# Gate products in three bf16 passes and weight rings of four tiles in a two-layer encoder with expert retrieval

## What is computed

```python
h = rmsnorm(x, norm_ffn[l]) * (1.0 + sc2) + sh2        # h: 256 x 1024
q = (h @ w_q).reshape(t, 8, 2, 128)                    # 8 heads, 2 sides
sc = einsum('thpd,hpnd->thpn', q, sub_keys)            # 128 keys a side
v1, i1 = top_k(sc[:, :, 0], 16); v2, i2 = top_k(sc[:, :, 1], 16)
cand = v1[..., :, None] + v2[..., None, :]             # 16 x 16 a head
top_v, top_pos = top_k(cand, 16)                       # expert = i1 * 128 + i2
gates = softmax(top_v)
a = gelu(einsum('tkd,td->tk', u_tab[eidx], x)) * gates
out = einsum('tk,tkd->td', a, v_tab[eidx])             # 16384 experts in u, v
x = x + g2 * out
```

## Time and profile before

| | us |
|---|---|
| median of 3 runs | 2061.69 |
| lowest and highest | 2059.86, 2061.74 |
| the profiled execution | 2065.37 |
| its span, first to last instruction | 2063.4 |
| mean granted TensorE clock | 0.987 of full speed |

### The profile page before, as it was taken

One profiled execution on the slowest core, in us unless ns is written; L12 is line 12 of the kernel. 1 busy time (PEld: TensorE's weight loads), 2 busy tenths in 40 slices (PEclk: granted clock), 3 DMA queues, 4 the chain that ended last, 5 costly groups with the idle time before them and its releaser, 6 DMA issues.

```text
span 2063.4 us, 43464 instructions
## 1 busy us (share of the span) xinstructions
PE 2018.4 (98%) x12678; PEld 1805.7 (88%) x12678; DVE 1487.8 (72%) x3743; ACT 1054.8 (51%) x2059; POOL 27.7 (1%) x56
## 2 busy tenths in 40 slices
PE   7989999999999999999999999999999999999997
PEld 6748899999999877777779689999999998888886
DVE  5662778877777688888875348786777767777776
ACT  2032245755555555555544424566555555555554
POOL 0000000000000000000000000000000000000000
PEclk9999999999999999999989999999999999999998
DMA  9861288865655899999820333777565577777774
GB/s 377 343 236 46 87 279 288 251 189 177 175 171 175 277 325 327 322 328 323 279 102 31 154 117 121 229 219 212 172 176 175 171 207 245 242 240 241 241 242 150
DMA packets 170904, 446.79 MB, mean 217 GB/s; under 512 B 19024, under 2 KB 85840, under 8 KB 166880
## 3 DMA queue, kind: packets, MB, share of 16 engines
q1 hardware_dynamic: 163472, 392.65, 59.6%
q0 software_dynamic: 7376, 53.45, 6.6%
HBM read 409.32 MB, written 36.70 MB: 216 GB/s over the span
## 4 chain that ended last, share of the span: by engine, by line
PE 94%; ACT 2%; DVE 2%; DMA 1%; issue 1%; DVEq 0%; ACTq 0%; SPq 0%
PE bank L492 93%; ACT big L931 1%; DMA big<-in_w_mod 1%; PE bank L631 1%; DVE raw L1097 0%; DVE big L1192 0%; PE bank L811 0%; DMA cst<-in_consts 0%; DVE big L1114 0%; DVE wmod_ring L1114 0%; DVE x_lo L1106 0%; DVE big L1527 0%; ACT L991 0%; ACT big L949 0%; ACT raw L878 0%
## 5 line engine op out<-in xcount | busy, mean ns | idle before, releaser
L1356 DVE TENSOR_TENSOR lo<-raw,hi 128x512 fp32r<-128x512 f32 x1024 | 702.5, 690 | 346.4 <-ACT hi L985 342.1
L985 ACT ACTIVATE hi<-raw 128x512 fp32r<-128x512 f32 x1024 | 642.8, 630 | 444.1 <-PE bank L492 430.2
L492 PE MATMUL bank<-x_hi,hi 128*128 128x256 f32 x2152 | 622.2, 289 | 3.9 <-ACT x_hi L876 1.8
L492 PE MATMUL bank<-x_hi,lo 128*128 128x256 f32 x2152 | 610.1, 283 | 0.0
L492 PE MATMUL bank<-x_lo,hi 128*128 128x256 f32 x2152 | 606.1, 283 | 0.0
L492 PEld LDWEIGHTS bank<-x_hi,hi 128*128 128x128 f32 x2152 | 413.6, 192 | 6.8 <-issue 4.2
L492 PEld LDWEIGHTS bank<-x_hi,lo 128*128 128x128 f32 x2152 | 413.6, 192 | 0.0
L492 PEld LDWEIGHTS bank<-x_lo,hi 128*128 128x128 f32 x2152 | 411.7, 192 | 0.0
L492 PE MATMUL bank<-hi,a_hi 128*128 128x512 f32 x1024 | 401.3, 392 | 3.4 <-issue 1.7
L492 PE MATMUL bank<-hi,a_lo 128*128 128x512 f32 x1024 | 398.8, 389 | 0.0
L492 PE MATMUL bank<-lo,a_hi 128*128 128x512 f32 x1024 | 398.4, 389 | 0.0
(11 more groups left out here) (159 smaller groups left out, 1344.4 us busy)
## 6 DMA issues: line engine op xcount, KB each, us to landing
raw<-in_u SPq DMA_DIRECT2D x256, 512.0 KB, 3.9
raw<-in_v SPq DMA_DIRECT2D x256, 512.0 KB, 4.6
s_store<-work SPq DMA_DIRECT2D x256, 128.0 KB, 3.7
wmod_ring<-s_store SPq DMA_DIRECT2D x256, 128.0 KB, 3.7
wmod_ring<-in_w_mod SPq DMA_DIRECT2D x54, 512.0 KB, 5.7
big<-in_w_mod SPq DMA_DIRECT2D x40, 512.0 KB, 6.3
big<-in_w_q POOLq DMA_DIRECT2D x16, 1024.0 KB, 7.1
big<-in_w_in POOLq DMA_DIRECT2D x6, 2048.0 KB, 14.4
```

Of the source, the lines that this page charges most:

```text
L492: return nc.tensor.matmul(o, w, x, start=start, stop=stop, skip_group_check=free)
L985: f(hi[:, r % 2, c], raw[:, r, c], ACT.Copy).then_inc(s[l]["hi_done"], 1)
L1356: v.tensor_tensor(lo[:, r % 2, c], raw[:, r, c], hi[:, r % 2, c].bitcast(F32), ALU.subtract).then_inc(s[l]["lo_done"], 1)
```

## The change

1. **Gate products in bf16.** The gate of each token is written as a sum of three bf16 numbers (`gate_bf`), indices are kept in bf16 (`pick_bf`). VectorE writes the one-hot of the second index for four tokens with the token innermost (`hot_second`), the one-hot of the first in bf16 (`hot_first`), and `hot_second` times the three parts (`hot_gate`, 1536 elements). TensorE multiplies three times for each token, reading `hot_gate` with a step of four elements. `iota4` is a constant that is written once.
2. **Rings of four tiles.** `hi` and `lo` are four deep, and split and remainder work on whole tiles of 1024, three tiles ahead of TensorE's use in the ring. `advance` after each remainder has 1000 (300 with a dot product) in place of twice 500.
3. **Layer 1's projection.** The first three tiles are multiplied in plain fp32; `x_hi` and `x_lo` are made beside them, and only then the split tiles follow.
4. **Layer 0's first weights.** The first piece of w_in is halved: 1 MB after four dot products, 1 MB after 15, the next piece after 16.
5. POOL's DMA scratch is set to 2048 bytes.

```diff
-SPLITS = 2
+SPLITS = 4
+PLAIN_TILES = 3
-                    for n in range(4):
-                        last = mm(bank[b][:, n * P:(n + 1) * P], hot[b % 2][:, 0, n, :], hot[b % 2][:, 1, n, :])
+                    for n in range(4):
+                        for c in range(3):
+                            last = mm(bank[b][:, n * P:(n + 1) * P], hot_first[b % 2][:, n, :], hot_gate[b % 2][:, c, :, n], c == 0, c == 2)
...
-                        v.tensor_scalar(hot[r % 2][:, 1, n, :], iota, pick[:, 1, bass.ds(4 * g + n, 1)],
-                                              pick[:, 2, bass.ds(4 * g + n, 1)], ALU.is_equal, ALU.mult)
+                    if again:
+                        dve.wait_ge(s[l]["hot_ready"], g)
+                    v.tensor_tensor(hot_second, iota4, pick_bf[:, 1, bass.ds(4 * g, 4)].unsqueeze(1).to_broadcast([P, P, 4]), ALU.is_equal)\
+                        .then_inc(s[l]["hot_plain"], 1)
+                    v.tensor_tensor(hot_first[r % 2], iota.unsqueeze(1).to_broadcast([P, 4, P]),
+                                    pick_bf[:, 0, bass.ds(4 * g, 4)].unsqueeze(2).to_broadcast([P, 4, P]), ALU.is_equal)
+                    dve.wait_ge(s[l]["hot_plain"], g + 1)
+                    v.tensor_tensor(hot_gate[r % 2], hot_second.unsqueeze(1).to_broadcast([P, 3, P, 4]),
+                                    gate_bf[:, :, bass.ds(4 * g, 4)].unsqueeze(2).to_broadcast([P, 3, P, 4]), ALU.mult)\
+                        .then_inc(s[l]["hot_ready"], 1)
...
-                def split(n, r, h, round_, wait=True):
+                def split(n, r, round_, wait=True):
-                        act.wait_ge(s[l]["w_used"], 2 * n + h - 3)
-                    c = slice(h * HALF, (h + 1) * HALF)
-                    f(hi[:, r % 2, c], raw[:, r, c], ACT.Copy).then_inc(s[l]["hi_done"], 1)
+                        act.wait_ge(s[l]["w_used"], n - 3)
+                    f(hi[:, r], raw[:, r], ACT.Copy).then_inc(s[l]["hi_done"], 1)
...
-                    split(n + 2, nr, 0, nround)
+                    split(n + 3, (r + 3) % 4, round_ + (r + 3) // 4, wait or r > 0)
                     gelu(n, r, round_, wait)
-                    split(n + 2, nr, 1, nround)
...
                     weigh(j + 2, (r + 2) % 4, round_ + (r + 2) // 4)
-                    for half in range(2):
-                        lower(NKEY + 2 + j, (r + 2) % 4, half)
+                    if left:
+                        lower(NKEY + 3 + j, (r + 3) % 4)
                     lower_a(j + 2, r, (r + 2) % 4)
...
-                    sp.wait_ge(s[l]["lo_done"], STREAM - 6 + 2 * j)
+                    sp.wait_ge(s[l]["lo_done"], NKEY - 3 + j)
                     load_v(j, r)
                     if fetches:
                         fetch(j + 1, (r + 1) % 4, i + (1 if r == 3 else 0))
...
+                for m in range(PLAIN_TILES):
+                    weights_in(m)
+                    for k in range(KT):
+                        if m == 0:
+                            pe.wait_ge(norms["h_ready"], KT * 2 + k + 1)
+                        last = mm(bank[m][:, 0:T], w_qk(1, m, k), hT[:, k, :], k == 0, k == KT - 1)
+                    last.then_inc(s[1]["wt_used"], 1)
+                pe.wait_ge(s[1]["ph_done"], KT)
+                pe.wait_ge(s[1]["pl_done"], KT)
```

More of the change, by code:

```diff
@@ L183, in build @@
         fox_maps = wmod_ring[:].rearrange("p a n -> p (a n)")
-        hot = [x.rearrange("p (a t n) -> p a t n", a=2, n=P) for x in (wmod_ring[:, 0], wmod_ring[:, 1])]
+        hot_first = [ring[:, n * D:n * D + 256].bitcast(BF16).rearrange("p (t n) -> p t n", t=4) for n in range(2)]
+        hot_gate = [ring[:, n * D + 256:(n + 1) * D].bitcast(BF16).rearrange("p (a n t) -> p a n t", a=3, t=4) for n in range(2)]
         back = wmod_ring[:, 2].rearrange("p (r t) -> p r t", t=T)
@@ L1406, in experts @@
                         for n in range(2):
-                            for half in range(2):
-                                lower(n, n, half)
+                            lower(n, n)
                 for n in range(GROUP_AT - 2):
-                    for half in range(2):
-                        lower(n + 2, (n + 2) % 4, half)
-                        if l == 0 and half and n % MIX_STEP == 0 and n < MIX_STEP * MIXED_MODS:
-                            mixed_modulation(n // MIX_STEP)
-                        else:
-                            advance(500)
+                    lower(n + 2, (n + 2) % 4)
+                    if l == 0 and n % MIX_STEP == 0 and n < MIX_STEP * MIXED_MODS:
+                        mixed_modulation(n // MIX_STEP)
+                        advance(300)
+                    else:
+                        advance(1000)
                 for _ in left:
@@ L1432, in experts @@
                     for r in range(4):
-                        for half in range(2):
-                            lower(4 * i + r, r, half)
+                        lower(4 * i + r, r)
                 dve.wait_ge(s[l]["g_copied"], GROUPS)
@@ L1438, in experts, with down_step @@
                 for n in range(2):
-                    for half in range(2):
-                        lower(NKEY + n, n, half)
+                    lower(NKEY + n, n)
                     lower_a(n, n, n)
-                def down_step(j, r, round_, mods=None):
+                lower(NKEY + 2, 2)
+                def down_step(j, r, round_, mods=None, left=True):
                     weigh(j + 2, (r + 2) % 4, round_ + (r + 2) // 4)
-                    for half in range(2):
-                        lower(NKEY + 2 + j, (r + 2) % 4, half)
+                    if left:
+                        lower(NKEY + 3 + j, (r + 3) % 4)
                     lower_a(j + 2, r, (r + 2) % 4)
```

300 lines of the change are left out of this document (138 added, 162 removed).

## The result

| | before | after |
|---|---|---|
| median of the runs, us | 2061.72 (4 runs) | 2154.31 (4 runs) |
| lowest and highest | 2059.86, 2063.20 | 2148.68, 2158.88 |
| ratio of the medians, 95% interval | | 1.0448, 1.0422 to 1.0475 |
| span of the profiled execution | 2063.4 | 2152.5 |
| granted TensorE clock | 0.987 | 0.992 |

A forecast was written before the change was run, and what follows sets the result against it. TensorE, busy 98% of the span, was taken as the bound. Terms -16.1 - 8 - 2.6 - 2 = -28.7 us took the profiled 2065.4 to 2036.7; the median being 3.7 lower, 2033.0 us was predicted, range 2016 to 2064.

The forecast's parts named there:

- gate products: Gate steps on TensorE: 12 bf16 matmuls at 0.057 us replace 8 fp32 records, -16.1 us (ends -26 and +68).
- VectorE in the gate step: Gate step: VectorE needs 2.9 us at doubled bf16 pace, stays hidden behind TensorE's 3.63 us, costs nothing.
- ring, layer 0's down stage: Layer 0's down stage: four-deep ring bridges the dot-product gaps, -8 us (ends -11.8 and +4).
- start of layer 1: Layer 1's projection: three plain fp32 tiles let TensorE begin at once, -2.6 us (-0.9 to -4.3, depending on the clock).
- up to the first gate product: Start of layer 0: halved first w_in load leaves room for modulation weights, -2 us (ends 0 and -2.5).
- the picks' row: Profile row of 64 bf16 matmuls of 128 columns, 0.057 us each, taken as the pace of the new gate matmuls.
- Rival (c): Layer 0's down stage: late loads stall four tiles 1 us instead of 0.4, +19 us, total 2060 us; 6 in 100.
- if this stays: Layer 1's projection: if TensorE stays at 1.2 GHz in part, denser work loses 3.4 us, only 0.9 gained.
- (a): Gate step: the twelve matmuls run slower, halfway at 0.085 us, +14.3 us in all, 2076 us; 11 in 100.
- the far part of (a): Gate step: matmul spacing above about 0.077 us, which the predicted range left out.

The follow-up runs named there:

- both repairs: Changed kernel with two tokens innermost in the gate operand (4-byte step) and SyncE fetching row j-1, not j+1, behind load j: 2029.26 us, ratio 0.9841.
- the later fetch: Changed kernel, but in the down stage SyncE issues behind tile j's load the fetch of row j-1 instead of j+1: 2110.15 us, ratio 1.0233.
- the lead of two: Changed kernel with the ring of four kept, but weights split two tiles ahead instead of three: 2105.47 us, ratio 1.0216.

## Why the prediction was wrong

Its steps against the kernel after, and against the one with both repairs (marks as in the table above):

| step | predicted | after | both repairs |
|---|---|---|---|
| gate products | -16.1 | +62.3 | -17.8 |
| VectorE in the gate step | 0 | 0 | 0 |
| ring, layer 0's down stage | -8 (-11.8 to +4) | +34.9 | -11.8 |
| start of layer 1 | -2.6 (-0.9 to -4.3) | -6.5 | -7.4 |
| up to the first gate product | -2 (0 to -2.5) | -1.5 | -0.4 |
| the rest | 0 | +0.2 | +0.3 |

Each column is one execution. What the small terms are worth is seen from the ten profiles, the kernel after and the nine experiments, whose programs are all but the same up to the first gate product and from the last down product of layer 0 to the end of layer 1's projection. The first gate product starts between 430.3 and 434.4 (434.5 before), and from the last down product to layer 1's first projection matmul it takes 11.4 to 14.0 us (13.9 before). The two large terms are far outside such spreads, the last digits of the small ones are not.

**The gate products: the picks' row was applied to an operand that is read otherwise.** The prediction named the difference itself ("the new moving operand is read with a step of four elements"), had a rival for it at 11 in 100, and its upper end, 0.112 us and +68, was nearly met (0.108 and +62.3). What failed is the choice between the ends and the spacing inside the rival: halfway, 0.085, when what came was a clean halving. The row was right for contiguous rows (0.054), for 4 bytes of step (0.057) and for a stepped stationary operand (0.056); for 8 bytes of step in the moving operand there was no row. The Trainium skill ("SBUF — State Buffer", the passage on 16-byte lines), by which eight bf16 elements would be the limit, does not hold for TensorE's moving read: four elements cost double here. The Trainium skill's 81 ns a matmul ("TensorE: Matmul & The Clock Gate") was not met by either pace.

**VectorE: right.** The equality of 512 with fp32 input was expected at 0.60 us from start to start, the one in bf16 at 0.33, the product at 0.87; the timeline above has 0.60, 0.34 and 0.87. The doubled pace was taken from a one-source row, and two sources have it too, as the Trainium skill ("Vector Engine (DVE) Microarchitecture Reference", section 5.1) says. The trace agrees: 0.95 us for 1536 elements.

**The ring: the time that a load of v may take was set too high.** The step that failed is "the load may take three tiles less 0.8 us, 7.4 us ...; its median there is 5.8". In the turn shown above 4.75 us go to conversions and 1.2 to issues, which leaves about 4.9 us of 10.9 for the load, not 7.4. Loads of v took more: 6.93 and 6.25 us in that chain, 5.7 in the median from 800 to 1040. Layer 1 has the same order of loads and fetches; there they land after 4.4 us in the median, and nothing stalls. The median also hid that the loads are of two kinds: the one in four behind a w_mod load lands after 6.6 us in the median (30 loads in layer 0's down stage), the others after 4.9. These slow loads alone make no stall: they took 6.3 us with the later fetch and 6.6 with the lead of two, where the stage takes 347.5. A run without the w_mod load in front was not made. Rival (c) had this mechanism, its place and its sign right, at 6 in 100, and its price too small: it took 1 us for every four tiles, and it was (394.2 - 347.5) / 32 = 1.5. Once the load is issued in time, the ring gives all of the 11.8 us, not 8.

**The start of layer 1: sign right, size beyond the good end.** Of the 6.5 us, 4.8 lie in the projection (60.4 to 55.7 us), where 4.3 was the good end; from its first matmul to its last it takes 55.3 to 55.6 us in all ten profiles with the new order, and 60.1 before. The other 1.7 us lie ahead of it (13.9 to 12.2 us from the last down product). The clock's part is in these stretches of the kernel after (columns as in the earlier trace rows), beside 0.72 and 0.59 in the earlier trace rows:

```profile
1130.00:1135.00 5.00, 4.64 (x20) 3.59 (x19) 3.57 (x10) 3.98 (x11) 0.00 (x0) 0.82 0.00 2
1135.00:1140.00 5.00, 5.00 (x24) 4.39 (x24) 4.68 (x10) 4.87 (x10) 0.00 (x0) 1.00 0.00 0
```

The first plain matmul starts at 1131.67; from 1135 on the granted clock is that of 2.4 GHz, and the drop towards 1.2 GHz that the earlier trace rows have inside the projection does not come. The bad end, "if this stays", did not happen. The 1.7 us ahead of the projection can't be called an effect of the change: programs that are all but the same had 11.4 to 14.0 us there in the ten profiles, and the 13.9 before lies among them.

**The start of layer 0.** The first projection matmul comes at 33.65 instead of 36.40, 2.75 us earlier, a little more than the end of 2.5. In the ten profiles it comes between 33.57 and 34.80, so 1.6 us earlier at least. At the first gate product 1.5 us are left, and 0.4 in the kernel with both repairs; that mark spreads over 4.1 us in the ten profiles, so what is left there is not resolved, and where the rest goes was not tested. POOL's smaller scratch, costed at nothing, shows no cost: the 18 loads of w_in for layer 1 have 528 ns of POOL each in both kernels.

**The chances.** 25 of 100 lay on the rivals, each priced alone. What came was (a) and (c) together, near or beyond their worst, and the range had cut off "the far part of (a)". The two losses are independent, as the experiments show, and without them the gate products and the ring give what was forecast or more. With both repairs the kernel takes 2029.26 us, where 2033.0 had been predicted for the change as it stood. That nearness is in part luck: the ring and the start of layer 1 gave more than their terms, the start of layer 0 less.

## What to carry to other kernels

Before a layout is chosen for the engine that writes it, ask what step the engine that reads it gets: for a bf16 moving operand 4 bytes of step were free and 8 bytes halved the pace, and making the stepped operand the stationary one also removed the cost. When a consumer is moved ahead by a tile, walk the queue that feeds it entry by entry: what stands in front of the transfer, what that entry waits for, how long the slowest transfer of the pattern takes, not the median, and how much conversion and issue time lies between one load and the load that hangs on it. A rival with a known bad end deserves that end as its price, and two independent rivals deserve a case in which both come.

## What was not expected of the hardware

- TensorE, bf16, 128 columns: 0.108 us a matmul if the moving operand has a step of 8 bytes; 0.057 with 4 bytes, 0.054 without a step. Other steps were not run.
- The weight load doesn't share this: with a step of 8 bytes in the stationary operand the spacing of matmuls is 0.056 us.
- The prediction had counted on this from a one-source row alone: VectorE multiplies two bf16 sources at the doubled pace even where a source's inner row has two elements and is repeated: 550 ns by groups for 768, as here:

```profile
L1359 DVE TENSOR_TENSOR wmod_ring<-wmod_ring 128x768 bf16<-128x768 bf16 x256 | 130.4, 550 | 0.0
```
